# A 64 bytes smaller filler tile ahead of the stage buffers of a two-layer decoder kernel

## The chip, the cores and the metric

The kernel runs on one core of a Trainium2 chip. The metric is the device time of one execution in microseconds, median of several; the kernel before takes 1511.85 us.

## The reference

Two decoder layers over 256 tokens of width 1024, all in float32. Each layer has a mixer (an mLSTM branch and an attention branch, gated and projected back) and then a feed-forward part: a dense SwiGLU of width 2816 in the first layer, and in the second one SwiGLU of width 3584 for each of 8 experts, of which every token uses two.

```python
for layer in range(DEPTH):
    h = rms_norm(x, mix_norm_g[layer])
    x = x + hybrid_mixer(h, ...)              # projections, mLSTM, attention, gates, w_out
    h = rms_norm(x, ffn_norm_g[layer])
    if layer % 2 == 0:
        x = x + swiglu(h, dense_w_gate, dense_w_up, dense_w_down)
    else:
        x = x + moe_swiglu(h, router_w, expert_w_gate, expert_w_up, expert_w_down)

def moe_swiglu(h, router_w, wg, wu, wd):      # (8, 1024, 3584) x 2, (8, 3584, 1024)
    gates = ...                               # softmax over the top 2 of 8 logits
    for e in range(N_EXPERTS):
        y = y + gates[..., e:e+1] * swiglu(h, wg[e], wu[e], wd[e])
```

## The kernel before, in words

**Weights.** Every weight matrix is read once from HBM, in pieces of 128 partitions x 1024 floats (512 KB). SyncE's queue issues the loads in the order of use. In the mixers and in the dense stage a load brings two pieces into a sixth of the tile `raw` (12 pieces, lines 314 to 315). In the expert stage a load brings one piece, into a ring of `RING` = 21 slots (`raw_slot`, lines 317 to 321): slots 0 to 11 are the halves of `raw`, slots 12 to 18 are the tile `more`, slots 19 and 20 are the tile `toep`, which held the attention bias until then. A slot is loaded again as soon as its piece has been used (`slot_free`, line 442). A gate or up piece is two rows of 2048 bytes in each partition, a down piece one row of 4096 bytes (lines 465 to 471).

**Split and matmul.** A piece is split for TensorE into two parts, `w_hi` (ScalarE, line 1265) and `w_lo` (VectorE, line 1630), with six buffers of each. `piece` (line 618, its matmul on line 627) then takes three matmuls for each tile: activation high part by `w_hi`, high by `w_lo`, low by `w_hi`. The stationary operand of these, 128 x 128, is the activation, the moving one is 512 columns of the weight. Only in the first two chunks of a mixer (`swap`) it is the other way round: the weight is stationary and 256 columns of `hT_hi` or `hT_lo` move. Which tile the activation lies in depends on the stage: `hT_hi`, `hT_lo` in the mixers' projections and in the experts' gate and up pieces; `g_hi`, `g_lo` in the mixers' branch projections (line 912) and in the dense stage's gate and up pieces; `aT_hi`, `aT_lo` in the dense stage's down pieces; `ex_hi`, `ex_lo` in the experts' down pieces.

**Expert jobs.** The experts are taken in 8 jobs of 84 pieces, 352 MB in all. Jobs 0, 1, 3, 5 and 7 are wide: 128 gathered tokens, each piece split as above, six matmuls a piece. Jobs 2, 4 and 6 are narrow: up to 64 tokens, and TensorE reads the float32 piece straight from its ring slot (lines 1183 and 1193), with `x_narrow` or `act_narrow` as the stationary operand.

**Where the tiles lie.** Tiles are laid out in each partition one after the other in the order of their calls, each on a multiple of 32 bytes. A nameless tile `to_line` (line 140) brings `raw` to byte 16896, a multiple of 512; `w_hi`, `w_lo`, `x`, `hT_hi`, `hT_lo`, `cst` and `toep` follow, and each starts at a multiple of 512 too. Small tiles follow, then `rbc`, and then the nameless `to_line2` (line 171), of 480 bytes, which starts at byte 158816. Behind it, from byte 159296 = 311 x 512 + 64, the stage buffers share the space: `g_hi`, `g_lo` with the mixers' or the dense stage's tiles (`aT_hi`, `aT_lo`, `sg`, `act`), and later the experts' tiles (`ex_hi`, `ex_lo`, `ex_act`, `x_narrow`, `act_narrow`, `more`, `xg_rows`, `y_rows`). All of the expert stage's tiles and all of `g_hi`, `g_lo`, `aT_hi`, `aT_lo`, `qk` and `v` start 64 bytes past a multiple of 512; the mixers' tiles behind `v` (4128 bytes) start 96 bytes past one.

Of the kernel before, what the change touches and what calls it, by code (L numbers as in the profile page):

```python
# [12 lines left out]
P = 128  # L13
# [114 lines left out]
def program(nc, x_in, rel_bias, mix_norm_g, w_in, conv_w, conv_b, igate_b, fgate_b, mlstm_norm_g,  # L128
# [3 lines left out]
    with ExitStack() as ctx:  # L132
        def sb(name, shape, dt=F32):
            return ctx.enter_context(nc.sbuf_tensor(name, shape, dt))
# [33 lines left out]


        rbc = sb("rbc", [P, S])  # L170
        sb("to_line2", [P, 120])
        halves_of = ExitStack()
        g_hi, g_lo = [halves_of.enter_context(nc.sbuf_tensor(n, [P, A, D], F32R)) for n in ("g_hi", "g_lo")]
        mix = ExitStack()
# [2105 lines left out]
```

## Time and profile before

| | |
|---|---|
| median of 3 runs | 1511.85 us (1511.79 to 1512.26) |
| the profiled execution | 1511.59 us, of which its span 1509.8 us |
| TensorE | busy 96% of the span |
| VectorE, ScalarE, GpSimd | 65%, 55%, 2% |
| read from HBM | 457.68 MB |
| chain that ended last | TensorE 84%, DMA 5%, VectorE 5%, ScalarE 3% |

The span is the time from the first to the last instruction; 1.8 us of the execution lie around it. Stages are told apart by their windows: first mixer to 204 us, dense stage to 399 us, second mixer and routing to 600 us, then the eight jobs. The chain of waits is followed back from the last instruction, at each step to what released it; in order of time it gives runs of matmuls that followed each other without a break, with their number, from which a pace can be worked out more finely than from the duration of one matmul, since matmuls overlap.

### The profile page before, as it was taken

Reading aid. Unit: us, or ns where it says so; the run is one execution under the profiler, and the core shown is the slowest. Engines: PE = TensorE matmul, PEld = TensorE weight load, DVE = VectorE, ACT = ScalarE, POOL = GpSimd, SP = SyncE. Lnnn points to the kernel's source line nnn. Section 1 sums busy time; section 2 is a strip of 40 time slices with the busy share of each in tenths; the row PEclk is TensorE's granted clock in tenths of the full one; section 3 lists DMA queues with packets and bytes.
Section 4 is the critical chain, followed back from the end, with each engine's and each line's share of the span. In section 5 each row is a group of like instructions: output and inputs, shape, how many; then the busy total and the mean of one; then the engine's idle time right before and its main releaser. Section 6 shows DMA issues by size and latency. Waiting matters only on the chain.

```text
span 1509.8 us, 20323 instructions
## 1 busy us (share of the span) xinstructions
PE 1448.8 (96%) x6996; PEld 1073.4 (71%) x6996; DVE 980.3 (65%) x1306; ACT 835.9 (55%) x1084; POOL 36.7 (2%) x48
## 2 busy tenths in 40 slices
PE   9999999999999999999999988999887999888998
PEld 8887888888888777788888423888323888325787
DVE  5878665445587866998998202998104988105997
ACT  6657564344665756777877102776002876004885
POOL 2000010000000000000000000000000000000000
PEclk9999999999999999999999999999999999999999
DMA  9544475555455548899999999999999999999995
GB/s 359 189 141 168 151 270 193 178 185 167 140 167 168 168 167 293 307 398 367 367 388 372 337 404 411 405 399 411 407 410 409 405 401 411 402 409 410 405 409 203
DMA packets 207507, 466.13 MB, mean 309 GB/s; under 512 B 13288, under 2 KB 15600, under 8 KB 207408
## 3 DMA queue, kind: packets, MB, share of 16 engines
q1 hardware_dynamic: 203376, 452.50, 80.5%
q0 software_dynamic: 3856, 12.25, 2.2%
q8 instruction: 61, 1.00, 0.3%
q14 instruction: 38, 0.31, 0.1%
q10 hardware_dynamic: 176, 0.07, 0.0%
HBM read 457.68 MB, written 7.09 MB: 308 GB/s over the span
## 4 chain that ended last, share of the span: by engine, by line
PE 84%; DMA 5%; DVE 5%; ACT 3%; issue 2%; SPq 1%; ACTq 0%; DVEq 0%
PE pA L627 57%; PE pB L627 8%; PE pA L1183 8%; PE pA L1193 4%; DMA raw<-expert_w_up_dram 2%; PE pB L651 2%; DVE w_lo L1630 2%; SPq L470 1%; ACT w_hi L1265 1%; DMA raw<-expert_w_gate_dram 1%; PE pA L651 1%; DMA more<-expert_w_up_dram 1%; DMA more<-expert_w_gate_dram 1%; ACT ex_act L1594 1%; PE pB L1202 1%
## 5 line engine op out<-in xcount | busy, mean ns | idle before, releaser
L1630 DVE TENSOR_TENSOR w_lo<-raw,w_hi 128x1024 fp32r<-128x1024 f32 x426 | 501.3, 1219 | 111.4 <-ACT w_hi L1265 108.4
L1265 ACT ACTIVATE w_hi<-raw 128x1024 fp32r<-128x1024 f32 x426 | 432.0, 1057 | 123.1 <-PE pA L627 48.3
L627 PE MATMUL pA<-w_hi,hT_hi 128*128 128x512 f32 x848 | 337.7, 398 | 11.8 <-DVE w_lo L1630 11.7
L627 PE MATMUL pA<-w_hi,hT_lo 128*128 128x512 f32 x848 | 331.7, 391 | 0.0
L627 PE MATMUL pA<-w_lo,hT_hi 128*128 128x512 f32 x848 | 331.6, 391 | 0.0
L627 PEld LDWEIGHTS pA<-w_hi,hT_hi 128*128 128x128 f32 x848 | 159.9, 189 | 50.6 <-DVE w_lo L1630 16.3
L627 PEld LDWEIGHTS pA<-w_hi,hT_lo 128*128 128x128 f32 x848 | 159.9, 189 | 34.2
L627 PEld LDWEIGHTS pA<-w_lo,hT_hi 128*128 128x128 f32 x848 | 160.1, 189 | 31.4
L2193 DVE TENSOR_TENSOR ex_act<-pA,ex_act 64x512 f32<-64x512 f32 x21 | 14.6, 694 | 246.4 <-ACT ex_act L1594 246.4
L1630 DVE TENSOR_TENSOR w_lo<-more,w_hi 128x1024 fp32r<-128x1024 f32 x140 | 165.7, 1219 | 11.6 <-ACT w_hi L1265 9.4
L1265 ACT ACTIVATE w_hi<-more 128x1024 fp32r<-128x1024 f32 x140 | 147.0, 1060 | 39.2 <-PE pA L627 31.0
L1594 ACT ACTIVATE ex_act<-pA 64x512 f32<-64x512 f32 x21 | 12.4, 589 | 216.9 <-PE pA L1183 216.9
L1183 PE MATMUL pA<-raw,x_narrow 128*64 128x512 f32 x432 | 109.1, 596 | 1.7 <-DMA more<-expert_w_up_dram 1.4
L627 PE MATMUL pA<-w_hi,ex_hi 128*128 128x512 f32 x272 | 108.0, 397 | 0.0
L627 PE MATMUL pA<-w_lo,ex_hi 128*128 128x512 f32 x272 | 107.6, 395 | 0.0
L627 PE MATMUL pA<-w_hi,ex_lo 128*128 128x512 f32 x272 | 107.5, 395 | 0.0
L627 PE MATMUL pA<-w_hi,g_hi 128*128 128x512 f32 (+1 forms) x224 | 85.3, 381 | 0.0
L627 PE MATMUL pA<-w_hi,g_lo 128*128 128x512 f32 (+1 forms) x224 | 84.6, 378 | 0.0
L627 PE MATMUL pA<-w_lo,g_hi 128*128 128x512 f32 (+1 forms) x224 | 84.5, 377 | 0.0
L1183 PEld LDWEIGHTS pA<-raw,x_narrow 128*64 128x64 f32 x432 | 32.7, 137 | 55.6 <-issue 55.0
L627 PEld LDWEIGHTS pA<-w_hi,ex_lo 128*128 128x128 f32 x272 | 51.2, 188 | 12.3
L627 PEld LDWEIGHTS pA<-w_lo,ex_hi 128*128 128x128 f32 x272 | 51.2, 188 | 12.0
(386 smaller groups left out, 1782.6 us busy)
## 6 DMA issues: line engine op xcount, KB each, us to landing
raw<-expert_w_down_dram SPq DMA_DIRECT2D x131, 512.0 KB, 11.0
raw<-expert_w_gate_dram SPq DMA_DIRECT2D x129, 512.0 KB, 11.2
raw<-expert_w_up_dram SPq DMA_DIRECT2D x124, 512.0 KB, 10.9
more<-expert_w_up_dram SPq DMA_DIRECT2D x87, 512.0 KB, 11.0
raw<-w_in_dram SPq DMA_DIRECT2D x43, 1024.0 KB, 5.0
more<-expert_w_gate_dram SPq DMA_DIRECT2D x74, 512.0 KB, 11.1
more<-expert_w_down_dram SPq DMA_DIRECT2D x63, 512.0 KB, 11.3
toep<-expert_w_down_dram SPq DMA_DIRECT2D x30, 512.0 KB, 11.5
```

Source lines behind the costliest of these rows:

```text
L470: sp.dma_start(raw_slot(EX0 + r).rearrange("p (k n) -> p k n", k=1 if kind == "down" else 2), src).then_inc(e_loaded[r % RING], 16)
L627: ins = mm(o, r if swap else l, l if swap else r, start=first and n == 0, stop=True, skip_group_check=True)
L651: return mm(o, src, ident, is_transpose=True, start=first, stop=True, skip_group_check=True)
L1183: ins = mm(bank[NARROW * n:NARROW * (n + 1), :], x_narrow[:, 2 * q + k, :], src[:, COLS * k:COLS * (k + 1)], start=(q == 0 and k == 0), st ...
L1193: ins = mm(B2[NARROW * n:NARROW * (n + 1), :], act_narrow[:, c % 2, q, :], src[:, COLS * n:COLS * (n + 1)], start=(c == 0 and q == 0), sto ...
L1202: ins = mm((B4, B5)[c % 2][:, NARROW * k:NARROW * (k + 1)], ex_act[NARROW:, c % 2, P * k:P * (k + 1)], ident[NARROW:, NARROW:], is_transpo ...
L1265: f(w_hi[:, m % PARTS, :], raw_slot(m), ACT.Copy).then_inc(s["w_hi_done"], 1)
L1594: f(ex_act[NARROW:, c % 2], (B0, B1)[c % 2][0:NARROW, :], ACT.Silu).then_inc(s["n_silu_done"], 1)
L1630: tt(w_lo[:, m % PARTS, :], raw_slot(m), w_hi[:, m % PARTS, :].bitcast(F32), ALU.subtract).then_inc(s["w_lo_done"], 1)
L2193: tt(ex_act[NARROW:, c % 2], (B0, B1)[c % 2][NARROW:, :], ex_act[NARROW:, c % 2], ALU.mult)\
```

## The change

The nameless tile `to_line2` gets 104 floats instead of 120, so it is 416 bytes long instead of 480. Everything behind it lies 64 bytes lower. `g_hi`, `g_lo`, `qk`, `v`, `aT_hi`, `aT_lo`, `sg`, `act` and all the expert stage's tiles, `more` with its seven ring slots among them, then start at multiples of 512 bytes; the mixers' tiles behind `v` start 32 bytes past one instead of 96. No instruction is added, removed or moved.

```diff
         rbc = sb("rbc", [P, S])
-        sb("to_line2", [P, 120])
+        sb("to_line2", [P, 104])
         halves_of = ExitStack()
```

## Rows read from the trace of the kernel before

**Rows 1.** The page: GB/s moved in 40 equal slices of the span.
```profile
GB/s 359 189 141 168 151 270 193 178 185 167 140 167 168 168 167 293 307 398 367 367 388 372 337 404 411 405 399 411 407 410 409 405 401 411 402 409 410 405 409 203
```

**Rows 2.** Windows, one for each of jobs 1, 2, 4, 5: length, engines, clock, DMA share, GB/s.
```profile
723.70:843.80 120.10, 120.10 (x548) 98.41 (x548) 105.05 (x106) 88.78 (x96) 2.63 (x2) 1.00 1.01 378
843.80:940.30 96.50, 82.00 (x383) 28.17 (x383) 14.04 (x35) 12.03 (x22) 2.79 (x3) 0.98 1.01 389
...
1060.70:1161.40 100.70, 81.56 (x384) 27.83 (x384) 16.10 (x37) 11.80 (x21) 3.15 (x3) 1.00 1.04 409
1161.40:1284.50 123.10, 123.10 (x547) 100.60 (x547) 104.88 (x105) 87.95 (x94) 1.65 (x1) 0.98 1.04 406
```

**Rows 3.** Groups of instructions: low-part matmuls of 512 columns, by stationary tile.
```profile
L627 PE MATMUL pA<-w_hi,hT_lo 128*128 128x512 f32 x848 | 331.7, 391 | 0.0
...
L627 PE MATMUL pA<-w_hi,ex_lo 128*128 128x512 f32 x272 | 107.5, 395 | 0.0
...
L627 PE MATMUL pA<-w_hi,g_lo 128*128 128x512 f32 x192 | 75.7, 394 | 0.0
...
L627 PE MATMUL pB<-w_hi,aT_lo 128*128 128x512 f32 x88 | 34.7, 394 | 0.0
```

**Rows 4.** Chain in order of time: start us, length us, unbroken runs of matmuls.
```profile
21.59 5.75 PE pA L627 x48
...
40.97 27.32 PE pA L627 x120
...
234.27 16.80 PE pA L627 x72
...
369.32 8.18 PE pA L627 x72
```

**Rows 5.** Timeline of TensorE in job 5: start us, duration us.
```profile
1230.08 0.40 PE L627 MATMUL pA<-w_hi,ex_lo 128*128 128x512 f32 x1
...
1237.78 0.39 PE L627 MATMUL pA<-w_hi,ex_lo 128*128 128x512 f32 x1
...
1239.40 0.39 PE L627 MATMUL pA<-w_hi,hT_hi 128*128 128x512 f32 x1
...
1244.61 0.39 PE L627 MATMUL pA<-w_hi,hT_lo 128*128 128x512 f32 x1
```

**Rows 6.** DMA view, 868 to 1480 us, and one row of 640 to 720 us.
```profile
q1 hardware_dynamic: 106043, 242.38, 101.4%
...
more<-expert_w_up_dram SPq DMA_DIRECT2D x57, 512.0 KB, 11.4
...
more<-expert_w_up_dram SPq DMA_DIRECT2D x8, 512.0 KB, 6.6
```

**Rows 7.** Timeline of ScalarE in job 7: start, duration, [idle before <-releaser].
```profile
1396.62 1.06 ACT L1265 ACTIVATE w_hi<-more 128x1024 fp32r<-128x1024 f32 x1 [1.90 <-DMA more<-expert_w_up_dram]
...
1399.33 1.06 ACT L1265 ACTIVATE w_hi<-more 128x1024 fp32r<-128x1024 f32 x1 [0.30 <-DMA more<-expert_w_up_dram]
...
1404.64 1.06 ACT L1265 ACTIVATE w_hi<-more 128x1024 fp32r<-128x1024 f32 x1 [0.33 <-DMA more<-expert_w_gate_dram]
...
1408.33 1.06 ACT L1265 ACTIVATE w_hi<-raw 128x1024 fp32r<-128x1024 f32 x1 [0.15 <-DMA raw<-expert_w_down_dram]
...
1417.70 1.07 ACT L1265 ACTIVATE w_hi<-raw 128x1024 fp32r<-128x1024 f32 x1 [0.17 <-DMA raw<-expert_w_up_dram]
...
1422.77 1.06 ACT L1265 ACTIVATE w_hi<-raw 128x1024 fp32r<-128x1024 f32 x1 [0.20 <-DMA raw<-expert_w_gate_dram]
```

**Rows 8.** Windows in which `raw`, then `more` were loaded; columns as in rows 2.
```profile
1044.73:1060.09 15.36, 15.36 (x70) 12.50 (x70) 9.83 (x10) 6.62 (x7) 0.00 (x0) 1.00 1.05 408
...
1170.97:1180.36 9.39, 9.39 (x43) 7.79 (x42) 8.70 (x9) 7.64 (x8) 0.00 (x0) 1.00 1.05 398
```

**Rows 9.** Groups of instructions: ScalarE's split, from `raw` and from `more`.
```profile
L1265 ACT ACTIVATE w_hi<-raw 128x1024 fp32r<-128x1024 f32 x426 | 432.0, 1057 | 123.1 <-PE pA L627 48.3 <-PE pB L627 40.6 <-DMA raw<-expert_w_gate_dram 27.7
...
L1265 ACT ACTIVATE w_hi<-more 128x1024 fp32r<-128x1024 f32 x140 | 147.0, 1060 | 39.2 <-PE pA L627 31.0 <-DMA more<-expert_w_up_dram 5.8 <-DMA more<-expert_w_gate_dram 2.3
```

## The prediction

> **What bounds the kernel now.** I read the page first: TensorE is busy 96% of the span and most of the chain is its own, so up to the expert stage the pace of its matmuls sets the end. The GB/s slices say where that may stop being so: from about slice 24 on (868 us) they stand at about 400 to 411 [rows 1]. The DMA view of 868 to 1480 us agrees: the load queue's packets fill its sixteen engines (101%), and a load lands 11.4 us after its issue, where it took 6.6 us earlier, so nine loads stand in line [rows 6]. The windows by job show what that costs. Job 1 (wide) takes 120.1 us and job 2 (narrow) 96.5; the same work takes 100.7 in job 4 and 123.1 in job 5 [rows 2], 7.2 us more, and ScalarE's waits of 0.3 to 1.9 us for a DMA in job 7 [rows 7] are more of it. TensorE at its own pace needs (120.1 + 96.5)/2 = 108.3 us a job. The loads: 84 pieces are 44.04 MB, the queue moves 242.38 MB in 612 us [rows 6], 396 GB/s, so 111.2 us a job. The ring hides the difference of 2.9 us a job for two jobs, then TensorE waits. Two engines are bounds in turn, and the change touches what both read and write.
>
> **The change, part by part.** No instruction changes. What can change is the duration of instructions whose buffers move.
>
> *1. Split and elementwise work on moved tiles: nothing.* ScalarE splits a piece in 1057 ns from `raw` (on a multiple of 512 bytes) and in 1060 ns from `more` (64 past one) [rows 9]. Even 3 ns on 140 pieces would be 0.4 us, on an engine that waits. At nothing.
>
> *2. Matmuls with a moved stationary tile, before the expert stage.* The groups show a difference by stationary tile: 391 ns with `hT_lo`, which lies on a multiple of 512, and 395, 394, 394 with `ex_lo`, `g_lo`, `aT_lo`, all 64 bytes past one [rows 3]. Durations overlap, so the pace comes from the unbroken runs of the chain: 120 matmuls with `hT` in 27.32 us, 227.7 ns each; 72 with `g` in 16.80 us, 233.3 ns each [rows 4]. The timeline shows it in one job, with the same weights buffers moving: with `ex`, 33 matmuls from 1230.08 to 1237.78 us, 233.3 ns; with `hT`, 23 from 1239.40 to 1244.61, 226.5 ns, and between them seven in 1.62 us, 231 ns [rows 5]. So `hT` matmuls settle into a faster rhythm after some six, and the others never do. Three tiles in different places share the slow pace and the offset; I take the offset as the cause, and the price as 233.3 - 227.7 = 5.6 ns (6.8 without the settling). The bounds: 0, if the place or the kind of piece is the cause, and 6.8.
> Matmuls of 512 columns concerned: branch projections 192, dense gate and up 480, dense down 264, together 936. 936 x 5.6 = 5.2 us, all in stages where TensorE is the bound. Against it: 96 matmuls of the last dense chunk move only 256 columns. They run at 8.18/72 = 113.6 ns with `g` 64 bytes off; the mixers' 256-column matmuls, both operands aligned, run at 5.75/48 = 119.8 ns [rows 4]. If aligned pairs behave alike, 96 x 6.2 = 0.6 us is lost, and I take that. Sum: -4.6 us (0 to -6.4).
>
> *3. Matmuls of the experts' down pieces.* 28 pieces of six in a wide job: 168 x 5.6 = 0.94 us a job. Jobs 0 and 1 come before the loads are the bound, so their 1.9 us bring everything after them forward. In jobs 3 and 5 it only makes TensorE wait longer for loads, and counts nothing. In job 7 the last waits for loads end near 1400 us [rows 7]; about 0.8 us of its gain stand behind them. Sum: -2.7 us (0 to -3.3).
>
> *4. Loads into `more`.* In job 7 ScalarE takes pieces as they land. Two intervals of `more` lie between 1396.62 and 1399.33, 1.355 us each; four of `raw` between 1417.70 and 1422.77, 1.268 us each, all gate or up pieces [rows 7]. That is 0.087 us more in `more`. Two windows, each cut at the landing of the last piece before a stretch and of its last piece, hold more of them: 12 gate and up pieces of `raw` in 15.36 us, 1.280 each, and seven of `more` in 9.39 us, 1.341 each, 0.061 more [rows 8]. But not all of that is lost: the three pieces after a `more` stretch (two of `toep`, one of `raw`) come within 1404.64 to 1408.33, 1.23 us each [rows 7], faster than the steady 1.268, as if data had been read ahead while the writes were held up. The GB/s of the windows say the same: 408 while `raw` is loaded, 398 while `more` is [rows 8], which is 524288/398 - 524288/408 = 32 ns a piece, 0.23 us for seven, the lower bound. The upper is 7 x 0.061 = 0.43 us. I take 0.28 us for each turn of the ring, near the lower bound because the catching up is seen. Where the loads are the bound, from 868 to about 1397 us, there are 529/27.8 = 19 turns (27.8 = 111.2/4): -5.3 us (-4.4 to -8.1). Behind 1397 the loads' gain reaches nothing that ends late.
> The Trainium skill has a rule for this ("DMA: Bandwidth & Descriptors", How a descriptor splits into AXI transactions): a descriptor that does not start on 256 bytes begins with a transaction from the boundary below it. Worked out as an estimate for a 2048-byte row 64 bytes off, that is 66 beats instead of 64, 3% or 0.04 us a gate or up piece; by it the sum would be some -4 us, and the trace shows more than that per piece.
>
> **Does the sum fit?** The loads would take 111.2 - 1.1 = 110.1 us a job, TensorE 108.3 - 0.5 = 107.8. The loads stay the bound, though TensorE gets earlier: the time taken out on its side would be 4.6, five jobs' 4.7 and the waits, 7.2 at least, together 16.5, more than the 12.6 of the sum, so it doesn't cut the sum. Sum: 4.6 + 2.7 + 5.3 = 12.6. From the profiled execution, 1511.6 - 12.6 = 1499.0; the median of the runs is 0.3 higher and so would the forecast be at most. I leave it at 1499.0.
>
> **The rivals.**
> *A, the forecast:* both mechanisms work, 1499.0; its own range, with the bounds of terms 2 to 4, is 1495 to 1502. Chance 0.60.
> *B, only the loads gain.* The 227 ns rhythm belongs to `hT` for another reason (its place below byte 139776, or column pieces against row pieces). For it: `hT_hi` and `hT_lo` are the only aligned stationary tiles with 512 columns, and they lie side by side, so offset and place aren't told apart. Against it: `g` in column pieces is as slow as `ex` and `aT` in row pieces. Then 1511.6 - 5.3 = 1506.3. Chance 0.17.
> The Trainium skill speaks for this case ("TensorE: Matmul & The Clock Gate", Step-by-step: what each phase is for): weights are loaded through a read port of their own, without taking bandwidth from the running matmul, so an address of the stationary tile should not matter. The trace's 233.3 against 227.7 ns is not explained by it.
> *C, only the matmuls gain.* The slow loads of `more` come from its place, not its offset. Then 4.6 + 2.7 = 7.3: 1504.3. Against it: `toep`, elsewhere but aligned, lands at 1.23 us a piece [rows 7]. Chance 0.08.
> *D, neither:* both are matters of place, or the compiler's addresses are not what matters: 1511.6. Chance 0.10.
> *E, slower.* The 256-column rows are the true sign: aligned against aligned costs 6.2 ns more, and at 512 columns too, `hT` being fast for another reason. Then the terms of matmuls turn: 936 x 6.2 = 5.8, the 0.6 for the 96, jobs 0 and 1 2.1, job 7 0.9, together +9.4, less 5.3 if the loads gain: 1515.7; if they don't, 1521.0. It decides when a moved matmul gets more than 5 ns slower. Against it: at 512 columns the only aligned pairs of the trace are the fast ones. Chance 0.05.
>
> **How the numbers follow.** A is the likeliest, so 1499.0. The range reaches from 1494.5 (A with the highest price in each term: 6.4 + 3.3 + 8.1 = 17.8 is 1493.8, cut a little since TensorE would be the bound again from some 16.5 on) to 1507.5, which takes in B and C and leaves out D and E with 0.15. Changes below 0.2%, 3 us, can't be told from none. Faster: A, B, C, 0.85. Same: D, 0.10. Slower: 0.05.
>
> **What would show it.** Term 2: the dense stage's runs of 72 matmuls in 16.4 us instead of 16.80, the last chunk's in 8.6 instead of 8.18, job 0 starting 4 to 6 us earlier. Term 3: job 1 in 119.2 us. Term 4: windows of `more` at 408 GB/s, landings in `more` 1.28 us apart for gate and up pieces, the queue near 400 GB/s. Term 1: 1057 to 1060 ns for both splits. The loads should still be the bound in jobs 4 to 7. I am wrong if the runs with `g` keep 233 ns, or if `more` keeps 1.35 us, or if the loads gain and the waits don't shrink.

## The result and the profile after

| | before | after |
|---|---|---|
| median of 4 runs each | 1511.82 us (1511.61 to 1512.26) | 1499.12 us (1498.87 to 1499.19) |
| span of the profiled execution | 1509.8 us | 1497.3 us |

The ratio of the times is 0.9915, with a 95% interval from 0.9898 to 0.9932: 12.7 us faster, where 12.6 were forecast, and 1499.0 us was the predicted time.

The page of after, GB/s in 40 slices of the span, to be laid beside [rows 1]:
```profile
GB/s 354 189 149 172 143 273 203 180 186 175 137 168 169 170 168 295 306 397 374 370 392 371 342 410 412 410 402 412 409 412 409 411 405 411 412 411 411 411 411 212
```
The slices of the expert jobs stand at 409 to 412 where they stood between 399 and 411, with two dips left instead of several.

The chain of waits of after, in order of time (start us, length us, what): runs of matmuls without a break, which answer to [rows 4]:
```profile
41.37 27.33 PE pA L627 x120
...
157.74 11.15 PE pA L627 x48
...
233.47 16.34 PE pA L627 x72
...
365.09 8.63 PE pA L627 x72
```
The same stretches of before that are not among its rows above:
```profile
157.32 11.40 PE pA L627 x48
...
1505.05 1.20 PE pA L1117 x8
```
`hT` keeps its 27.33/120 = 227.8 ns. `g` in the dense stage goes from 233.3 to 16.34/72 = 226.9 ns, the 48 of a branch projection from 11.40/48 = 237.5 to 11.15/48 = 232.3. The last chunk's 72 matmuls of 256 columns take 8.63 us instead of 8.18, 119.9 ns instead of 113.6: they got slower.

Groups of after, first the matmuls by stationary tile (to [rows 3]), then both splits (to [rows 9]); the last two numbers of each row are us in all and ns of one:
```profile
L627 PE MATMUL pA<-w_hi,hT_lo 128*128 128x512 f32 x848 | 331.1, 390 | 0.0
...
L627 PE MATMUL pA<-w_hi,ex_lo 128*128 128x512 f32 x272 | 105.9, 389 | 0.0
...
L627 PE MATMUL pB<-w_hi,aT_lo 128*128 128x512 f32 x88 | 34.3, 389 | 0.0
```
```profile
L1265 ACT ACTIVATE w_hi<-raw 128x1024 fp32r<-128x1024 f32 x426 | 432.6, 1057 | 115.4 <-PE pA L627 44.4
...
L1265 ACT ACTIVATE w_hi<-more 128x1024 fp32r<-128x1024 f32 x140 | 147.0, 1061 | 36.5 <-PE pA L627 28.7
```
The difference between the stationary tiles is gone (389 and 390, before 391 against 394 and 395). The splits are as they were.

One group of matmuls has operands whose distance changes too, and its time did not change at all: those of the narrow jobs, which read the float32 piece from its ring slot. With `x_narrow` as the stationary operand, 64 bytes off, and `raw` moving, the first 48 of job 2 took 10.45 us before; after, with both aligned, they take 10.45 us again (from 836.89 us on), and 10.45 us in every other run below.
```profile
843.77 10.45 PE pA L1183 x48
```

ScalarE's timeline of after in job 7 (start, duration, [idle before <-releaser]): the last piece of a stretch of `more` and the third piece behind it, then the first and last of seven gate and up pieces of `more`. It answers to [rows 7].
```profile
1393.20 1.06 ACT L1265 ACTIVATE w_hi<-more 128x1024 fp32r<-128x1024 f32 x1 [0.29 <-DMA more<-expert_w_gate_dram]
...
1396.99 1.06 ACT L1265 ACTIVATE w_hi<-raw 128x1024 fp32r<-128x1024 f32 x1
...
1412.74 1.06 ACT L1265 ACTIVATE w_hi<-more 128x1024 fp32r<-128x1024 f32 x1 [0.22 <-DMA more<-expert_w_gate_dram]
...
1420.45 1.06 ACT L1265 ACTIVATE w_hi<-more 128x1024 fp32r<-128x1024 f32 x1 [0.22 <-DMA more<-expert_w_up_dram]
```
The same stretch of `more` in before, its first and its sixth piece:
```profile
1424.14 1.06 ACT L1265 ACTIVATE w_hi<-more 128x1024 fp32r<-128x1024 f32 x1 [0.30 <-DMA more<-expert_w_gate_dram]
...
1430.84 1.06 ACT L1265 ACTIVATE w_hi<-more 128x1024 fp32r<-128x1024 f32 x1 [0.26 <-DMA more<-expert_w_up_dram]
```
Six intervals in 7.71 us are 1.285 us each, near the 1.268 of `raw`; in before the five of this stretch took 6.70 us, 1.340 each (the two of [rows 7] 1.355).

Windows of after by job (length, engines, granted clock, DMA share, GB/s): jobs 1, 2, 4 and 5, to [rows 2].
```profile
717.80:836.80 119.00, 119.00 (x546) 98.39 (x544) 105.45 (x106) 88.84 (x96) 2.64 (x2) 1.00 1.01 382
836.80:935.10 98.30, 83.83 (x384) 28.78 (x383) 14.00 (x35) 13.91 (x23) 2.75 (x3) 0.97 1.01 392
...
1055.90:1152.40 96.50, 82.10 (x384) 28.36 (x384) 13.94 (x35) 11.79 (x21) 2.67 (x3) 0.98 1.04 410
1152.40:1271.60 119.20, 119.20 (x547) 98.51 (x547) 106.34 (x107) 88.50 (x94) 2.13 (x2) 1.00 1.04 409
```
Job 2 begins 7.0 us earlier (836.8, was 843.8). Jobs 4 and 5 took 100.7 and 123.1 us and take 96.5 and 119.2, almost what jobs 1 and 2 take without waiting for loads. Of job 5's gain, though, 2.8 us are no waits. TensorE was busy in all of the 123.1 us before. It had stood idle for 4.75 us ahead of them (2.43 in after), its granted clock then fell for 6.8 us to the lower level (1.2 GHz), and the first 108 matmuls took 27.62 us instead of 24.78. Whether the longer idle time brought the fall on is not shown. First the window in before (granted clock 0.57) and the run, then the run in after:
```profile
1160.00:1168.00 8.00, 6.61 (x17) 5.19 (x18) 6.04 (x6) 5.29 (x5) 0.00 (x0) 0.57 1.05 405
```
```profile
1161.39 27.62 PE pA L627 x108
```
```profile
1152.40 24.78 PE pA L627 x108
```

To price the loads by themselves, one window from the landing of job 3's first piece to that of job 7's, 336 pieces or 16 turns of the ring, in before and in after:
```profile
934.90:1377.90 443.00, 408.35 (x1870) 255.70 (x1866) 241.40 (x282) 199.91 (x230) 9.61 (x8) 0.99 1.04 406
```
```profile
927.40:1366.80 439.40, 409.26 (x1873) 256.44 (x1873) 241.08 (x283) 200.10 (x230) 9.61 (x8) 0.98 1.04 409
```
The loads begin the window 7.5 us earlier and end it 11.1 us earlier: 3.6 us in 16 turns, 0.225 us a turn.

### The profile page after: what moved, and what is told of

The parts are those of the page before. It is cut to its first block, busy times and chain, and to the rows that moved or that the text cites. A ratio compares the mean times of both kernels' runs of the same rounds, so it can differ in the third digit from the quotient of the medians.

```text
span 1497.3 us, 20323 instructions
## 1 busy us (share of the span) xinstructions
PE 1440.3 (96%) x6996; PEld 1073.0 (72%) x6996; DVE 979.1 (65%) x1306; ACT 836.3 (56%) x1084; POOL 36.7 (2%) x48
## 4 chain that ended last, share of the span: by engine, by line
PE 85%; DVE 5%; DMA 3%; ACT 3%; issue 2%; SPq 1%; ACTq 0%; DVEq 0%
PE pA L627 56%; PE pA L1183 9%; PE pB L627 8%; PE pA L1193 5%; PE pB L651 2%; DVE w_lo L1630 2%; SPq L470 1%; ACT w_hi L1265 1%; PE pA L651 1%; DMA more<-expert_w_gate_dram 1%; DMA raw<-expert_w_up_dram 1%; DMA more<-expert_w_up_dram 1%; ACT ex_act L1594 1%; PE pB L1202 1%; DVE act_narrow L2188 0%
## 5 line engine op out<-in xcount | busy, mean ns | idle before, releaser
L1265 ACT ACTIVATE w_hi<-raw 128x1024 fp32r<-128x1024 f32 x426 | 432.6, 1057 | 115.4 <-PE pA L627 44.4
L1265 ACT ACTIVATE w_hi<-more 128x1024 fp32r<-128x1024 f32 x140 | 147.0, 1061 | 36.5 <-PE pA L627 28.7
L1594 ACT ACTIVATE ex_act<-pA 64x512 f32<-64x512 f32 x21 | 12.4, 589 | 218.6 <-PE pA L1183 218.6
```

Of the source, the lines that this page charges most:

```text
L1265: f(w_hi[:, m % PARTS, :], raw_slot(m), ACT.Copy).then_inc(s["w_hi_done"], 1)
L1594: f(ex_act[NARROW:, c % 2], (B0, B1)[c % 2][0:NARROW, :], ACT.Silu).then_inc(s["n_silu_done"], 1)
```

## The experiments

Each kernel computes the same; only addresses differ. Each was timed in 2 to 10 executions; where their times lie more than 2 us apart this is said. Offsets are bytes past a multiple of 512. The time of before in the comparisons was 1511.88 us (first four), 1511.65 us (raw and the offsets of 32, 128 and 256 bytes) and 1511.9 us (the last two).

**1. Only the ring slots `more` aligned (e1_more_on).** From after, `g`, `aT`, `ex` and the other tiles that matmuls read are put back to 64; `more` stays at 0, and so do `xg_rows` and `y_rows` behind it, which take the gathered rows (2.5% of the load traffic in the DMA view).
```diff
         halves_of = ExitStack()
+        halves_of.enter_context(nc.sbuf_tensor("off_g", [P, 16], F32))
...
+        eb("off_ex", [P, 16])
         ex_hi = eb("ex_hi", [P, 2, 4, P], F32R)
...
-        act_narrow = eb("act_narrow", [P, 2, 4, NARROW])
+        eb("to_more", [P, 496])
         more = eb("more", [P, RING - 2 * RAW - 2, PIECE])
-        eb("behind_more", [P, 3 * PIECE])
+        eb("off_narrow", [P, 16])
+        act_narrow = eb("act_narrow", [P, 2, 4, NARROW])
+        eb("behind_more", [P, 3 * PIECE - 528])
```


> Only the ring slots in more (and the tiles behind it) lie on multiples of 512 bytes; g, aT, ex and x_narrow, act_narrow stay 64 bytes past one, as in the kernel before. If the two gains of the forecast are separate, this one has the loads' gain alone: gate and up pieces land in more 1.28 us apart instead of 1.34, matmuls with g and ex keep 233 ns, and the time is about 1506.3 us, 5.3 below the kernel before. If the slow loads belonged to the place of more and not to its offset, or if the waits for loads had shrunk only because TensorE was earlier, more keeps 1.34 us or the time stays at 1511.8.

Measured: 1508.16 us, ratio 0.998 (0.997 to 0.999), 3.7 us less than before, where 5.3 were expected. The ten executions scatter from 1506.83 to 1509.41, with one at 1514.72 that no trace explains. The chain of waits, with its shares by engine, and the window of 336 pieces:
```profile
PE 90%; DVE 5%; ACT 3%; issue 2%; DMA 0%; ACTq 0%; DVEq 0%
```
```profile
234.22 16.80 PE pA L631 x72
...
1351.19 5.35 PE pA L1197 x16
...
1501.77 1.23 PE pA L1121 x8
```
```profile
934.00:1373.60 439.60, 410.44 (x1862) 256.12 (x1860) 240.89 (x282) 199.55 (x230) 9.61 (x8) 0.98 1.04 409
```
The matmuls keep the slow pace (233.3 ns), and the loads gain all that they gain in after: 439.6 us, job 7's first piece 4.3 us earlier (1373.6 against 1377.9). But the last matmuls of the chain start only 3.3 us earlier (1501.77 against 1505.05). The share of DMA in the chain, 5% before, is 0%: in this execution TensorE is the bound to the end, and 1.0 us of the loads' gain doesn't pass through. Two things make TensorE late, and the run doesn't tell them apart: the slow pace of its matmuls, and drops of its granted clock. The 16 matmuls at 1351.19 us took 5.35 instead of 3.65 us, and a second drop followed at 1368.6; job 6 has a granted clock of 0.96. By these two alone TensorE is 3.4 us later, and job 7's first matmul starts 5.1 us after its piece has landed, where it took 2.5 us before. The other 1.0 us that is missing from the 5.3 of term 4 is the price of a turn, below.

**2. Only the matmul tiles aligned (e2_more_off).** From after, `more` (with what lies behind it, and the mixers' tiles from `so` on) is put back to where it lay.
```diff
         v = mb("v", [P, A, MH, MD + 1])
+        mb("off_so", [P, 16])
...
+        eb("off_more", [P, 16])
         more = eb("more", [P, RING - 2 * RAW - 2, PIECE])
```


> The counterpart: g, aT, ex, x_narrow and act_narrow lie on multiples of 512 bytes, more and what is behind it stays 64 past one. Theory of two separate gains: the dense stage's runs of 72 matmuls take 16.35 us, more still takes 1.34 us a gate or up piece, and the time is about 1504.3 us, 7.3 (4.6 + 2.7) below the kernel before. The two kernels' gains should add to the 12.7 that was measured for both. If the matmuls' pace came from traffic into more and not from the stationary tile's offset, g and ex would be back at 233 ns in the expert stage.

Measured: 1503.20 us, ratio 0.9945 (0.9928 to 0.9961), 8.7 us less. Chain, ScalarE's timeline in job 7 (first and last of six pieces of `more`), and the window:
```profile
233.05 16.34 PE pA L629 x72
...
1496.96 1.22 PE pA L1119 x8
```
```profile
1417.16 1.06 ACT L1267 ACTIVATE w_hi<-more 128x1024 fp32r<-128x1024 f32 x1 [0.29 <-DMA more<-expert_w_gate_dram]
...
1423.86 1.06 ACT L1267 ACTIVATE w_hi<-more 128x1024 fp32r<-128x1024 f32 x1 [0.27 <-DMA more<-expert_w_up_dram]
```
```profile
927.40:1370.90 443.50, 407.72 (x1860) 255.95 (x1858) 241.00 (x282) 199.56 (x230) 9.63 (x8) 0.98 1.04 407
```
The pace is after's, `more` takes 6.70/5 = 1.34 us a piece, and the window is as long as in before (443.5 against 443.0). So each gain comes from its own tiles, and the two, 8.7 and 3.7 us, make 12.4 of the 12.7; beside aligned matmuls (from this run to after) the loads' gain is 4.1 us. Rivals B, C and D fall: both paces changed with a shift of 64 bytes in the same place. Rival E falls too, since the matmuls with `g` of 512 columns got faster.

**3. The fast stationary tile put off (e3_hT_off).** After, with the 64 bytes of `gbias` ahead of `hT_hi`; `table` and `experts` (448 bytes) behind `hT_lo` bring what follows back to 0 (the small tiles behind `toep` shift too; the runs with `g` show no effect of it).
```diff
+        gbias = sb("gbias", [P, NL, 2 * MH])
         hT_hi = sb("hT_hi", [P, KT, S], F32R)
         hT_lo = sb("hT_lo", [P, KT, S], F32R)
+        table = sb("table", [P, A, 3, JOBS])
+        experts = sb("experts", [P, JOBS], I32)
```


> The kernel after with hT_hi and hT_lo alone moved to 64 bytes past a multiple of 512 (three small tiles are allocated around them; all else lies as in the kernel after). Offset theory: the 2736 matmuls of 512 columns with hT go from 227.5 to 233.3 ns, some 6 us before the expert stage (1056 of them), 1.9 us in each of jobs 0, 1 and 7, so about 1510.5 us. Place theory (hT is fast for where it lies): nothing, 1499.1. For the 384 matmuls of 256 columns in which hT moves and the weight is stationary: 120 ns if only the stationary tile's offset counts, 113.5 if the offset between the two operands does (that would give back 2.5 us).

Measured: 1508.59 us, 9.5 us more than after, where about 11 were expected; the eight executions lie between 1507.85 and 1511.35, and the trace is that of the slowest. Its chain:
```profile
21.27 5.66 PE pA L627 x48
...
40.47 28.10 PE pA L627 x120
...
234.47 16.35 PE pA L627 x72
```
`hT` now takes 28.10/120 = 234.2 ns (it took 227.8), in the same place but for 64 bytes, while `g` keeps 227. Place is excluded; the offset makes the pace. The swapped matmuls, in which `hT` moves and the weight is stationary, go from 119.8 to 5.66/48 = 117.9 ns, neither the 120 nor the 113.5 that were expected. Here the stationary operand lies 64 bytes below the moving one, and experiments 4 and 6 give the other pieces.

**4. The moving operand put off (e4_w_off).** Before, with `gbias` ahead of `w_hi` and the 448 bytes behind `w_lo`: now `w_hi`, `w_lo`, `g`, `ex` and `aT` all lie at 64, and `hT` at 0.
```diff
         raw = sb("raw", [P, RAW, UNIT])
+        gbias = sb("gbias", [P, NL, 2 * MH])
         w_hi = sb("w_hi", [P, PARTS, PIECE], F32R)
         w_lo = sb("w_lo", [P, PARTS, PIECE], F32R)
+        table = sb("table", [P, A, 3, JOBS])
+        experts = sb("experts", [P, JOBS], I32)
```


> The kernel before with w_hi and w_lo moved to 64 bytes past a multiple of 512, where g, aT and ex lie too; hT, raw and the rest as before. If the stationary tile's own offset sets the pace: g, aT and ex keep 233.3 ns, hT keeps 227, and the time stays near 1511.8 us. If the offset between the stationary and the moving operand sets it: g, aT and ex go to 227 ns (-7.3 us) and hT, now 64 bytes below its moving operand, leaves the fast pace, up to +12 us, so 1504 to 1517 with the paces the other way round; the 96 matmuls of 256 columns with g go from 113.6 to 120 ns.

Measured: 1504.64 us, ratio 0.9953 (0.9937 to 0.9969). Its chain:
```profile
21.29 5.46 PE pA L627 x48
...
40.05 27.57 PE pA L627 x120
...
232.60 16.34 PE pA L627 x72
```
`g` runs at 226.9 ns although it lies where it lay before. So it is not the stationary tile's own offset that counts, as the prediction had it, but the distance between the two operands of a matmul: 64 and 64 is as good as 0 and 0. `hT`, now 64 bytes below the weights' offset, takes 229.8 ns, between the two paces. The swapped matmuls, whose stationary weight now lies 64 bytes above `hT`, take 5.46/48 = 113.8 ns, as the dense stage's with `g` 64 above the weights did (113.6).

**5. `raw` put off too (e5_raw_off).** Before, with 64 bytes ahead of `raw` and 448 behind it, so that 19 of the 21 ring slots lie at 64; no operand of a matmul of line 627 moves.
```diff
         sb("to_line", [P, 96])
+        gbias = sb("gbias", [P, NL, 2 * MH])
         raw = sb("raw", [P, RAW, UNIT])
+        table = sb("table", [P, A, 3, JOBS])
+        experts = sb("experts", [P, JOBS], I32)
```


> The kernel before with raw moved to 64 bytes past a multiple of 512 as well, so 19 of 21 ring slots (all but the two of toep) and every load before the expert stage lie off; all else keeps its offset. Offset theory: gate and up pieces land in raw 1.34 us apart too, and the catching up behind more is gone, so a turn of the ring takes some 19 x 0.064 = 1.2 us more than with all slots aligned and 0.9 us more than in the kernel before: about 20 turns are bound by loads, +18 us, 1530 us. If only the place of more were slow, raw keeps 1.28 us and the time stays at 1511.8. Matmuls keep their paces (227 with hT, 233 with g, aT, ex).

Measured: 1528.34 us, ratio 1.0111 (1.0082 to 1.0141). ScalarE at the start of job 7, then the window of 336 pieces:
```profile
1393.33 1.06 ACT L1265 ACTIVATE w_hi<-raw 128x1024 fp32r<-128x1024 f32 x1 [8.79 <-DMA raw<-expert_w_gate_dram]
1394.67 1.06 ACT L1265 ACTIVATE w_hi<-raw 128x1024 fp32r<-128x1024 f32 x1 [0.29 <-DMA raw<-expert_w_gate_dram]
1396.03 1.06 ACT L1265 ACTIVATE w_hi<-raw 128x1024 fp32r<-128x1024 f32 x1 [0.30 <-DMA raw<-expert_w_gate_dram]
```
```profile
937.10:1393.20 456.10, 414.89 (x1866) 257.78 (x1862) 241.61 (x282) 199.51 (x230) 9.63 (x8) 0.98 1.04 396
```
Pieces of `raw` now land 1.34 and 1.36 us apart, where the same three came 1.22 and 1.28 us apart before. The window is 13.1 us longer than before's for twelve more slots off, 0.82 us a turn; that is 0.068 us for each of these slots, where the seven of `more` alone cost 0.225/7 = 0.032 each. One reading is that with seven slots off fourteen others catch up and with nineteen off only two can; that is argued and not shown on its own. The last 19 turns at 0.82 make 15.6 us; the whole kernel lost 16.7. This is the loads' cost with TensorE's pace untouched.

**6. Other distances (off32, off128, off192, off256, off448).** After, with the filler of another length: everything behind it lies the named number of bytes past a multiple of 512. For 256:
```diff
-        sb("to_line2", [P, 104])
+        sb("to_line2", [P, 40])
```


> The kernel after with everything behind the filler tile at 32 bytes past a multiple of 512 instead of 0. Theory one (steps of 64 bytes matter, relative to the moving operand, since a stationary tile 64 bytes on gave 233 ns and both at 64 gave 227): either pace may come out; theory two (any offset but an equal one is slow): 233 ns for g, aT, ex. Loads: a row that starts off any boundary of 64 bytes or more is slow, 1.34 us in more. Time near that of the kernel before, 1511.8, if both are slow; 1503 if only the loads are.

> The same at 128 bytes past a multiple of 512. Loads: 1.28 us in more if a boundary of 128 bytes is enough for them, 1.34 if it takes 256 or 512. Matmuls: 227 ns if 128 bytes between the operands are as good as none, another pace if each step has its own. Time 1499 if both are fast, 1506 if only the loads are, 1503.5 if only the matmuls are, 1511.8 if neither.

> The same at 256 bytes past a multiple of 512. Loads: 1.28 us in more if 256 bytes are enough, which the skill's splitting rule would say, 1.34 if it must be 512. Matmuls as for 128: 227 ns, or a pace of its own. Time 1499 if both are fast, 1506 if only the loads are, 1511.8 if neither.

> All tiles behind the filler lie at 448 bytes past a multiple of 512, so 64 bytes below one. Theory 1 (only the distance modulo 256 between stationary and moving operand counts, and every distance but zero is slow): the dense stage's runs and the matmuls with ex keep 233 ns, the 256-column ones about 114 ns, `more` 1.35 us a gate or up piece, and the time is as before, 1510 to 1513 us. Theory 2 (the sign of the distance counts, as the 229.4 ns of hT suggest where the weights lay 64 bytes above it): with the stationary tile 64 bytes below the weights' line some 229 ns, loads as in theory 1, and 1511.9 - 6.5 x 4/6.5 = about 1508 us.

> All tiles behind the filler at 192 bytes past a multiple of 512. Theory 1 (period of 256 bytes): it should behave as the 448 of the run beside it, for matmuls and loads alike, whatever that one does. Theory 2 (a period of 512, with 256 fast by chance of its own): paces between those at 128 and at 256, so below 232 ns, and another time than at 448. Loads into `more` 1.35 us in both, 1.28 us only at 0 and 256.

The first runs of 72 matmuls with `g` in their chains, in the order 32, 128, 192, 256, 448, and the last chunk's 256-column run of off448:
```profile
233.70 16.79 PE pA L627 x72
```
```profile
233.80 16.73 PE pA L627 x72
```
```profile
234.23 16.50 PE pA L627 x72
```
```profile
233.37 16.34 PE pA L627 x72
```
```profile
233.56 16.50 PE pA L627 x72
...
366.31 8.48 PE pA L627 x72
```
The window of 336 pieces, as above, in off128 and in off256:
```profile
934.10:1377.20 443.10, 412.28 (x1862) 256.37 (x1860) 241.04 (x282) 200.22 (x230) 9.61 (x8) 0.98 1.04 407
```
```profile
927.00:1366.60 439.60, 409.29 (x1883) 256.64 (x1881) 241.23 (x283) 199.51 (x230) 9.60 (x8) 0.99 1.04 410
```

| offset | 0 (after) | 32 | 64 (before) | 128 | 192 | 256 | 448 |
|---|---|---|---|---|---|---|---|
| ns a matmul of 512 columns, dense stage | 226.9 | 233.2 | 233.3 | 232.4 | 229.2 | 226.9 | 229.2 |
| window of 336 pieces, us | 439.4 | 443.7 | 443.0 | 443.1 | 443.0 | 439.6 | 443.0 |
| median, us | 1499.12 | 1512.24 | 1511.82 | 1510.48 | 1505.8 | 1498.93 | 1506.16 |
| ratio to before | 0.9915 | 1.0005 | 1 | 0.9992 | 0.996 | 0.9917 | 0.9962 |

256 bytes do all that 512 do, for matmuls and loads, and 192 behaves as 448: the pattern repeats after 256 bytes. For the loads every offset but 0 and 256 costs alike, 3.6 to 4.3 us in the window. For matmuls the sign counts too: 64 bytes below the moving operand costs 2.3 ns, 64 above it 6.4. The times at 32 and 128 bytes (ratios 1.0005, 0.9994 to 1.0016, and 0.9992, 0.9981 to 1.0003) can't be told from before's. Of the expectation for off448, its second theory held for the pace, and its time of about 1508 was 2 us too high. It took 4 of 6.5 ns as vanishing, which is right, but of a gain of 6.5 us in all, where experiment 2 had measured 8.7. By the count of matmuls: 936 x 4.1 = 3.8 us, 336 x 4.1 = 1.4 in jobs 0 and 1 and 0.7 in job 7 make 5.9, less 0.4 for the 96 (8.48 us for 72 against 8.18), 5.5 of the 5.7 measured.

## Why the prediction was right, point by point

**What bounds the kernel.** Right in the main. TensorE sets the pace up to 868 us: experiment 2 moves everything before 868 and leaves the loads' window alone. Later the loads do: experiment 5 lengthens that window alone, and the kernel with it. Two things did not hold. After the change the loads should have been the bound in all of jobs 4 to 7; after's chain has loads in job 6 (from 1329 us on) and at the start of job 7 only, 3% of the span (5% before), and in jobs 4 and 5 TensorE. "They stay the bound, 110.1 against 107.8" stood nearer the edge than it looked, and experiment 1 lies beyond it. ScalarE's long wait for job 7's first piece tells nothing here: it is 8.55 us in after and 7.67 us in experiment 1, whose chain has no load. And of the 7.2 us that jobs 4 and 5 take longer than jobs 2 and 1, which the forecast put down to waits for loads, job 5's 3.0 are the lower clock shown above, which followed a wait and is none itself. The check of the sum stands without them: 16.5 - 3.0 = 13.5 is still more than 12.6.

**Term 1, the splits:** nothing, as said: 1057 and 1061 ns. The narrow jobs' matmuls, whose operands moved as well, stood in no term; that they are worth nothing (10.45 us for 48, before and after) was luck and not shown beforehand.

**Term 2, matmuls ahead of the experts.** The mechanism was right in what it does and mis-stated in what it is: the price goes with the distance between stationary and moving operand (experiment 4), not with the stationary tile's offset. Here the two are the same, since `w_hi` and `w_lo` lie at 0. The price was set at 5.6 ns, the slow pace against `hT`'s 227.7; `g` came down to 226.9, so it was 6.4, nearer the upper bound of 6.8. 936 x 6.4 - 0.6 = 5.4 us instead of 4.6; job 2 shows it together with jobs 0 and 1. The 96 matmuls of 256 columns lost 6.3 ns each, as taken. Rival E had the sign right for 256 columns and wrong for 512.

**Term 3, down pieces.** 168 x 6.4 = 1.1 us a job instead of 0.94. Job 1: 119.0 us, where 119.2 was to be seen. Job 2 begins 7.0 us earlier where 4.6 + 1.9 = 6.5 were forecast; by the measured price it would be 5.4 + 2.2 = 7.6. Of the 0.6 us between, the profiled execution was 0.4 us late already in the first mixer (41.37 against 40.97), and the 192 matmuls of the branch projections gained 5.2 ns each, not 6.4. With 1.1 us in job 7 terms 2 and 3 make 8.7 us, and experiment 2 measured 8.7.

**Term 4, the loads.** 0.225 us a turn, where 0.28 was taken and 0.23 was the lower bound: 19 turns make 4.3 us instead of 5.3. The lower bound was the better reading because it came from whole windows; the steady intervals leave out two things. First, what is caught up afterwards. That was not shown by the rows that the step used: the three pieces at 1.23 us were two down pieces of `toep` and one of `raw`, set against 1.268 us of gate and up pieces. The same three take at most 1396.99 - 1393.20 = 3.79 us in after, 3.69 in before, so at most 0.10 us is caught up in them. Second, every third piece is a down piece, whose rows are 4096 bytes long, and these lose less: in experiment 5, 64 bytes off, two pairs in `raw` landed 1.28 and 1.27 us apart (from 1456.66 and 1465.62 us on), in after aligned ones 1.24 us (from 1403.91 us on). A gate or up piece loses 1.340 - 1.285 = 0.055 us at the same place in the job, 0.07 by the two intervals at 1.355. An estimate from these: two thirds of seven slots at 0.055 to 0.07 us and one third at 0.035 are 0.34 to 0.41 us a turn, less 0.10 caught up 0.24 to 0.31, near the 0.225 measured.

**The sum.** Terms 2 and 3 were 1.4 us too small and term 4 1.0 us too large: 8.7 + 4.3 = 13.0 against 12.7 measured; where the last 0.3 went was not traced. That 12.6 and 12.7 agree to 0.1 us is luck, the two errors cancelling, and not the precision of the terms.

**The rule of the Trainium skill on a split at 256 bytes** ("DMA: Bandwidth & Descriptors", How a descriptor splits into AXI transactions) gives the right boundary: off256 is as fast as after. By the estimate worked out from it, 3% or 0.04 us a gate or up piece, the cost would be smaller than the traces' 0.055 to 0.07 us, 4 to 5%; the measurement decides. **The rule of the Trainium skill that weights come through a read port of their own** ("TensorE: Matmul & The Clock Gate", Step-by-step: what each phase is for) gives no reason for the tiles' addresses to matter. The runs don't agree: experiments 3 and 4 change nothing but addresses, and by them the same matmuls with their weight loads take 226.9 to 234.2 ns.

## What to carry to other kernels

Print the byte address of every large tile. Where loads are the bound, put each of their destinations on a multiple of 256 bytes, and give the stationary and the moving tile of a matmul the same offset modulo 256. Both cost at most 224 bytes of filler, since tiles start on multiples of 32, and here 64 bytes were worth 12.7 us. For matmuls this was measured with 128 x 128 stationary and 512 moving columns; with 256 columns the equal offset is the slowest of those tried (119.9 ns against 113.6 to 118.8), and the narrow float32 matmuls take 10.45 us for 48 at every offset. When two engines are bounds in turn, a gain on one of them passes through only while the other keeps up: run each half alone before adding them. And a job that takes longer where loads are late need not have spent the time waiting: look at its granted clock too.

## What the runs showed of the hardware that was not expected

- **The distance between the operands of a matmul sets its pace**, with a period of 256 bytes: 226.9 ns at 0, 233.2 at +32, 233.3 at +64, 232.4 at +128, 229.2 at +192 (or -64), for 128x128 stationary and 512 columns of float32 in two parts each. At 256 columns it is the other way: 119.9 ns at 0, 113.6 at +64, 8.48/72 = 117.8 at -64; the swapped matmuls of the mixers, with the weight as the stationary operand, agree (119.8, 113.8 and 117.9). Why is open: no run tells what in TensorE's reading of the two makes it.
- **Short stretches of a low clock** in the narrow jobs and right behind them. After's chain shows the same 16 matmuls in 3.65 us and in 5.35 us, and the window round the slow ones a granted clock of 0.69, which is 3.4 of 5.5 us at the lower level (1.2 GHz) and the rest at 2.4 GHz:
```profile
853.56 5.35 PE pA L1193 x16
...
868.46 3.65 PE pA L1193 x16
```
```profile
853.50:859.00 5.50, 5.44 (x18) 2.11 (x20) 1.34 (x7) 0.00 (x0) 0.00 (x0) 0.69 1.03 413
```
TensorE had been working through narrow matmuls with short pauses before each. One costs 1.7 us of TensorE's time; before's chain has one such run of 16 in job 2, after's job 2 two, which is why that job took 98.3 us instead of 96.5. Between 840 and 1380 us the traces hold 2 such drops in before (the one at 1160.6 twice as long), 6 in after, 7 in e1_more_on, 4 in e2_more_off, 6 in e5_raw_off and 3 in off192, one execution each. What their number depends on was not tried. Where TensorE is the bound they count in full, and differences of a microsecond or two between such kernels, and the scatter of experiments 1 and 3, may be theirs.
